# Weight halves at multiples of 512 bytes, and the first projection in another order of chunks with the compressed product's slabs between them

## The reference

```python
def hybrid_layer(h, w_in, ...):
    t = jnp.arange(S)
    hn = rms_norm(h, attn_pre_norm)
    proj = hn @ w_in                                   # 512 x 1024 @ 1024 x 2072
    (q_n, k_c, v_c, k_s, v_s, k_w, v_w, g_n, q_w, k_sw, v_sw) = jnp.split(proj, IN_SPLITS, axis=-1)
    qn = rope(kvh(q_n, NSA_HEADS), t).reshape(B, S, NSA_KV, NSA_GROUP, HEAD_DIM)
    k_c, k_s, k_w = (rope(kvh(z, NSA_KV), t) for z in (k_c, k_s, k_w))
    ckv = jax.vmap(compress)(jnp.stack([k_c, v_c]), cmp_pos, cmp_w1, cmp_w2)
    o_cmp, p_cmp = compressed_attention(qn, ckv[0], ckv[1], t)
    ...
    o_win = banded_attention(qn, k_w, v_w, NSA_WINDOW, None)
    gates = jax.nn.sigmoid(g_n)...
    qw = rope(kvh(q_w, SWA_HEADS), t)...
    kw = rope(kvh(k_sw, SWA_KV), t)
    o_swa = banded_attention(qw, kw, kvh(v_sw, SWA_KV), SWA_WINDOW, ...)
    mixed = jnp.concatenate([o_nsa, o_swa], axis=-1) @ w_out

def compress(kv, pe, w1, w2):       # overlapping blocks of 32 tokens: 31 blocks x 2 heads = 62 rows
    ...
    return jax.nn.gelu(flat @ w1) @ w2                 # flat: 62 x 2048, w1: 2048 x 256, for k and for v
```

## Time and profile before

| | |
|---|---|
| median of 3 runs | 2015.52 us (2012.99 to 2016.8) |
| the profiled execution: its time, its span | 2015.36 us, 2013.2 us |
| PE busy | 1911.2 us, 95% |
| PEld, DVE, ACT, POOL busy | 1519.0, 797.1, 470.6, 1081.5 us |
| mean granted clock of TensorE | 0.983 |
| chain that ended last | PE 86%, DVE 7%, ACT 4%, POOL 1%, DMA 1% |

### The profile page before, as it was taken

How to read it: one execution, slowest core, us unless ns; L and a number is a source line. 1 busy time by engine, 2 the same in 40 slices (tenths; PEclk the granted TensorE clock), 3 DMA queues, 4 the chain that set the end, 5 groups by cost and what they waited for, 6 DMA issues and landing times.

```text
span 2013.2 us, 28099 instructions
## 1 busy us (share of the span) xinstructions
PE 1911.2 (95%) x10416; PEld 1519.0 (75%) x10416; DVE 797.1 (40%) x1283; ACT 470.6 (23%) x1144; POOL 1081.5 (54%) x713
## 2 busy tenths in 40 slices
PE   8968899999999989988999999999998899999999
PEld 6857567888888877756888888887885688888887
DVE  5445655756662055663332232013527333222200
ACT  2115543322220043453210010011326221001000
POOL 7454125666665555252566666665534456666663
PEclk9988999999999999999999999999999999999999
DMA  4221012233232322210322332223221023332222
GB/s 160 76 88 33 2 33 84 84 95 93 94 104 84 101 72 77 62 44 22 95 92 93 93 94 94 92 79 85 84 63 34 32 84 94 94 94 94 94 94 84
DMA packets 121501, 159.50 MB, mean 79 GB/s; under 512 B 8514, under 2 KB 83778, under 8 KB 121409
## 3 DMA queue, kind: packets, MB, share of 16 engines
q1 hardware_dynamic: 121409, 158.21, 25.6%
HBM read 155.04 MB, written 2.10 MB: 78 GB/s over the span
## 4 chain that ended last, share of the span: by engine, by line
PE 86%; DVE 7%; ACT 4%; issue 1%; POOL 1%; DMA 1%; SPq 0%; DVEq 0%; POOLq 0%; ACTq 0%
PE ps L814 25%; PE ps L815 25%; PE ps L816 25%; PE ps L1187 3%; PE ps L1160 1%; PE ps L829 1%; DVE p_turn L2298 1%; DVE nmax L2264 1%; PE ps L1234 1%; ACT dump L1524 1%; ACT tok L1764 1%; PE ps L962 1%; ACT xt_hi L1543 1%; PE ps L1264 1%; PE ps L1250 1%
## 5 line engine op out<-in xcount | busy, mean ns | idle before, releaser
L457 POOL TENSOR_TENSOR w_lo<-raw,w_hi 128x1024 fp32r<-128x1024 f32 (+1 forms) x256 | 606.5, 2369 | 21.3
L455 POOL TENSOR_SCALAR w_hi<-raw 128x1024 fp32r<-128x1024 f32 (+1 forms) x256 | 267.5, 1045 | 551.1 <-PE ps L816 515.6
L814 PE MATMUL ps<-xt_hi,w_hi 128*128 128x512 f32 (+2 forms) x1096 | 427.1, 390 | 0.9 <-ACT tok L1932 0.9
L815 PE MATMUL ps<-xt_lo,w_hi 128*128 128x512 f32 (+2 forms) x1096 | 426.3, 389 | 0.0
L816 PE MATMUL ps<-xt_hi,w_lo 128*128 128x512 f32 (+2 forms) x1096 | 426.2, 389 | 0.0
L814 PE MATMUL ps<-w_hi,xt_hi 128*128 128x512 f32 (+3 forms) x672 | 263.3, 392 | 18.5 <-DVE tok L2413 12.8
L815 PE MATMUL ps<-w_lo,xt_hi 128*128 128x512 f32 (+3 forms) x672 | 258.9, 385 | 0.0
L816 PE MATMUL ps<-w_hi,xt_lo 128*128 128x512 f32 (+3 forms) x672 | 258.9, 385 | 0.0
L2103 DVE TENSOR_TENSOR ps<-ps,gains 128x512 f32<-128x512 f32 x132 | 92.1, 698 | 395.3 <-PE ps L816 395.3
L814 PEld LDWEIGHTS ps<-xt_hi,w_hi 128*128 128x128 f32 (+1 forms) x1096 | 206.0, 188 | 48.7 <-POOL w_lo L471 1.3
L815 PEld LDWEIGHTS ps<-xt_lo,w_hi 128*128 128x128 f32 (+1 forms) x1096 | 205.9, 188 | 47.5
(11 more groups left out here) (318 smaller groups left out, 2203.7 us busy)
## 6 DMA issues: line engine op xcount, KB each, us to landing
raw<-in_w_up SPq DMA_DIRECT2D x88, 256.0 KB
raw<-in_l_w_gate SPq DMA_DIRECT2D x88, 256.0 KB
raw<-in_l_w_up SPq DMA_DIRECT2D x88, 256.0 KB
raw<-in_l_w_down SPq DMA_DIRECT2D x40, 512.0 KB
raw<-in_l_w_in SPq DMA_DIRECT2D x36, 512.0 KB
raw<-in_w_down SPq DMA_DIRECT2D x20, 512.0 KB
raw<-in_l_w_o SPq DMA_DIRECT2D x16, 512.0 KB
raw<-in_w_in SPq DMA_DIRECT2D x12, 512.0 KB
```

The costliest lines, as they stand in the source:

```text
L455: e.tensor_scalar(w_hi[:, s, 0:width], r, 1.0, 0.0, ALU.mult, ALU.add).then_inc(split, 1)
L457: e.tensor_tensor(w_lo[:, s, 0:width], r, w_hi[:, s, 0:width].bitcast(F32), ALU.subtract).then_inc(split, 1)
L814: e.matmul(o, s_hi, m_hi, start=start, stop=False)
L815: e.matmul(o, s_hi, m_lo, start=False, stop=False)
```

## The change

1. Tensors. A tensor `align_h` of 384 bytes stands ahead of `h`, `rot` moves to another place, and the filler `align_x` grows. `raw` now starts at byte 33,280, `w_hi` at 41,472 and `w_lo` at 57,856, all multiples of 512; the tensors from `m_table` on, `xt` and `hid` among them, stay where they were.
2. The chunks of the first projection come in the order: compressed and second keys and values (`C_KV`, 512), sliding-window keys and values (`C_SK`, 256), queries (`C_Q`, 512), sliding-window queries (`C_SQ`, 512), window keys and values with the gates (`C_WIN`, 280). The two short key chunks are staged in `mixed` (`tok_short`) instead of `tok`.
3. The eight slabs of the compressed product stand one by one behind slab 3 of `C_Q`, the four of `C_SQ` and the first three of `C_WIN`, in the programs of SP, POOL and PE.
4. Of the eight banks, four hold the tiles, three the turns, and bank 7 the compressed product. The turns are at other places, and those of `C_WIN` (two, written to `kk[:, 2:4]`) go into rounds 4 and 6 of the attention, their copies into rounds 5 and 7 of ACT.
5. In DVE's program the rows for the compressed product stand behind the turn of `C_KV`; the gates' three operations go into round 3 of the attention. In ACT's program the GELU and its table loads stand ahead of the copies of `C_WIN`.
6. The attention's start waits for two tiles of `C_WIN` (`in1_tok` 18), its round 1 for all four.

```diff
-ALIGN = 12
+ALIGN = 44
...
+    sb("align_h", [P, 96])
     h = sb("h", [P, NT, D])
...
     sb("align_x", [P, ALIGN])
-    rot = sb("rot", [P, 4 * ROPE])
...
-    IN1 = [(0, 512), (512, 512), (1024, 280), (1304, 512), (1816, 256)]
+    IN1 = [(512, 512), (1816, 256), (0, 512), (1304, 512), (1024, 280)]
+    C_KV, C_SK, C_Q, C_SQ, C_WIN = range(5)
+    CMP_SLABS = [(kv, s) for kv in range(2) for s in range(4)]
+    ORDER1 = []
+    for c in range(5):
+        for s in range(4):
+            ORDER1.append(("in", c, s))
+            if 11 <= len([x for x in ORDER1 if x[0] == "in"]) - 1 < 19:
+                ORDER1.append(("cmp", *CMP_SLABS[len([x for x in ORDER1 if x[0] == "cmp"])]))
+    N1 = {x: n for n, x in enumerate(ORDER1)}
...
-    TOK_BANKS = {"in1": EVEN, "in2": EVEN, "in3": HIGH}
-    TURN_BANKS = {"in1": ODD, "in2": ODD, "in3": LOW}
+    TOK_BANKS = {"in1": (0, 1, 4, 5), "in2": EVEN, "in3": HIGH}
+    TURN_BANKS = {"in1": (2, 6, 3), "in2": ODD, "in3": LOW}
...
+    def pe_in1(e, plan):
...
+        turned = {(C_Q, 0): C_KV, (C_Q, 2): C_SK, (C_SQ, 2): C_Q, (C_WIN, 2): C_SQ}
+        for n, (kind, c, s) in enumerate(ORDER1):
+            e.wait_ge(split, 2 * (n + 1))
+            if kind == "cmp":
+                compressed(c, s).then_inc(slab_used, 1)
                 continue
...
             for t in range(NT):
+                if s == 0 and c:
+                    e.wait_ge(*at("in1_tok", 4 * c - 3 + t))
+                m = tile(c, s, t)
+            m.then_inc(slab_used, 1)
+            if (c, s) in turned:
+                pe_turn(e, "in1", plan, turned[c, s], [at("in1_tok", 4 * turned[c, s] + 4)])
...
+        def banks_there():
+            e.wait_ge(*at("in1_tok", 20))
+            e.wait_ge(*at("in1_copy", 12))
+            turned_layer()
...
-        hooks = {1: turned_layer, 3: second_layer, 5: lambda: scores(0), 7: lambda: scores(1), 11: lambda: turned(0),
+        hooks = {1: banks_there, 4: lambda: window_key(0), 6: lambda: window_key(1), 8: window_there, 3: second_layer, 5: lambda: scores(0), 7: lambda: scores(1), 11: lambda: turned(0),
...
+        for step in (C_KV, C_SK, (C_KV,), "high", (C_SK,), (C_Q,), (C_SQ,), "layer", C_WIN):
...
+        for step in (C_KV, C_SK, (C_KV,), "rows", (C_SK,), C_Q, (C_Q,), C_SQ, (C_SQ,), C_WIN):
+            if step == "rows":
                 block_rows()
                 block_rows_low()
...
         hooks, variance = dve_cat()
+        hooks.setdefault(3, []).append(gates)
```

More of the change, by code:

```diff
@@ L347, in n_slot, with sp_group @@
         return SLOT[0] % 2
-    def sp_group(e, grp, slabs, stride=W, first=0):
+    def sp_group(e, grp, slabs, stride=W):
         STRIDE[0] = stride
-        for s, parts in enumerate(slabs, first):
+        for s, parts in enumerate(slabs):
             SLOT[0] = s
@@ L397, in _ @@
         e.dma_start(g_pre[:, :, :], A["g_pre"]).then_inc(sem("g_full"), 16)
[L398 to L411, removed]
+        for n, (kind, c, s) in enumerate(ORDER1):
+            if kind == "in":
+                parts, STRIDE[0] = two_kt(A["w_in"][0], *IN1[c])[s], W
+            else:
+                parts, STRIDE[0] = [(0, cols(A["cmp_w1"][0, c], 0, 256, slice(4 * s, 4 * s + 4)))], 256
+            SLOT[0] = n
+            sp_slab(e, n, parts)
+            if n == 1:
+                e.dma_start(smalls[:, :], A["smalls"]).then_inc(sem("small_full"), 16)
+                e.dma_start(pos_i[:, :], A["positions"]).then_inc(sem("small_full"), 16)
+                e.dma_start(table[:, :], A["table"]).then_inc(sem("small_full"), 16)
         for c in range(2):
@@ L697, in _ @@
         ph = phases
[L698 to L701, removed]
+        for n, (kind, c, s) in enumerate(ORDER1):
+            if kind == "in":
+                split_cols(e, n // 4, n % 4, 2, IN1[c][1])
+            else:
+                split_slab(e, n // 4, n % 4, SLAB)
         pool_first(e, {3 + 4 * s: (ph["out1"].g0, s) for s in range(4)})
@@ L821, in pe_turn, with tile, compressed @@
             for s, v in tok_waits:
                 e.wait_ge(s, v)
-        for i, (cc, (off, w, _, _), _, _) in enumerate(plan):
-            if cc != c:
+        for i in units:
+            pe_turn_unit(e, name, plan, i)
+    def pe_in1(e, plan):
+        def tile(c, s, t):
+            n = N1["in", c, s]
+            for k in range(2):
+                hi, lo = x_model(2 * s + k, t)
+                cs = slice(k * W, k * W + IN1[c][1])
+                m = mm3(e, bank(TOK_BANKS["in1"][t], IN1[c][1]), hi, lo, w_hi[:, n % 4, cs], w_lo[:, n % 4, cs],
+                        s == 0 and k == 0, s == 3 and k == 1)
+            if s == 3 and t < 3:
+                m.then_inc(sem("in1_acc"), 1)
+            return m
+        def compressed(kv, s):
+            n = N1["cmp", kv, s]
+            if s == 0:
+                e.wait_ge(*at("cmp_f", kv + 1))
+            for k in range(4):
+                pp = 4 * s + k
+                cs = slice(k * 256, (k + 1) * 256)
+                m = mm3(e, bank(7, 256, 256 * kv, 62), f_hi[:, kv, pp, :], f_lo[:, kv, pp, :], w_hi[:, n % 4, cs],
+                        w_lo[:, n % 4, cs], pp == 0, pp == CMPS - 1)
+            return m
+        turned = {(C_Q, 0): C_KV, (C_Q, 2): C_SK, (C_SQ, 2): C_Q, (C_WIN, 2): C_SQ}
+        for n, (kind, c, s) in enumerate(ORDER1):
+            e.wait_ge(split, 2 * (n + 1))
+            if kind == "cmp":
+                compressed(c, s).then_inc(slab_used, 1)
@@ L2420, in _, with rotate @@
         e.wait_ge(*od.latest())
-        for c in range(5):
+        def rotate(c):
             for t in range(NT):
```

177 lines of the change are left out of this document (92 added, 85 removed).

## The result

The changed kernel takes 1958.63 us (median of 4 runs, 1958.28 to 1962.69) where the kernel before takes 2014.26 in the same comparison (4 runs). The ratio is 0.9727, 95% interval 0.971 to 0.9745. The forecast was 1996.3, range 1986 to 2004: the direction held, the time did not. The change gained 55.6 us, not 19.1.

A forecast was written before the change was run, and what follows sets the result against it. TensorE was taken as the bound, working 1911 of 2013 us. 22.6 of waits + 4.2 of clock - 3.1 + 0.9 = 24.6, less 5.5 in the attention, gives 19.1; 2015.4 - 19.1 = 1996.3 us, range 1986 to 2004.

The forecast's parts named there:

- Part 4: Moving tensors to 512-byte starts gains 0; bounds: 63 us gained at a 213 ns step, or 6.9 us lost.
- starts quicken matmuls: Rival: starts at 512 speed up matmuls, 1989 us at 1 ns each, down to 1933; chance 0.08.
- slower: Rival: weights and activations 256 bytes apart modulo 512 collide more, 2024 us at 4 ns a matmul; chance 0.04.
- The order, 19.1 us: Whole forecast gain: 24.6 us won up to the attention less 5.5 us that the attention takes over.
- Waits removed, 22.6 us: PE's waits in the first 155 us: 12.8 for VectorE's tiles, 8.0 for compressed slabs, 1.8 the view hides.
- The clock at 105 to 122 us, 4.2 us: PE's work from 112.1 to 122.2 us ran at 1.2 GHz; at 2.4 GHz it takes 4.2 us less.
- No wait; the slack is 1 to 3 us: First query chunk: rows end at 72 us, its tiles rotate until 81.2, and PE gets its banks in time.
- Chunk 0 to 1, 1.0 and 1.1; the 280-wide chunk, 1.0: New PE waits for banks: two after the key/value chunk, one before the 280-wide chunk; 3.1 us in all.
- GpSimd and loads in the last chunk, no wait: Slabs between chunks: with three slabs of lead PE never waits for GpSimd; bound 0 to 3 us.
- The start of the attention, 2.9: First exponentials come 5.0 us after PE's projections instead of 2.1, behind table loads, copies and rotations: cost 2.9 us.
- Gates, evictions, transposes, 2.7: Work moved into the attention: gates 0.9 us, two window-key evictions 0.6, eight transposes 1.2.
- The clock stays up in the attention: Rival: the clock no longer falls early in the attention, worth some 6 us, so 1990 us; chance 0.17.

The follow-up runs named there:

- starts alone: The kernel before with only the tensors' places of the changed one, order of work as before: 1980.41 us, ratio 0.9829.
- slabs at the end: The changed kernel with the eight compressed slabs behind all five chunks and the GELU behind the last chunk's copies: 1967.1 us, ratio 0.9774.
- order alone: The changed kernel with the tensors where they were before, so only the order of work differs from the kernel before: 1994.95 us, ratio 0.9888.
- rows in two: The changed kernel with the keys' rows in place and the values' rows moved behind the first query chunk's rotation: 1957.14 us, ratio 0.972.
- the worst: The changed kernel with the rows in two parts and GELU with table loads behind the last chunk's copies: 1960.7 us, ratio 0.9731; attention 127.9 us.
- 32 apart: The changed kernel with raw, w_hi and w_lo 224 past a multiple of 512, xt and hid 256 past: 1995.27 us, ratio 0.9903.
- 64 apart: The changed kernel with raw, w_hi and w_lo 192 past a multiple of 512, xt and hid 256 past: 1985.30 us, ratio 0.9856.

## Why the prediction was wrong, point by point

- **Part 4, "I take 0, by these two": wrong, and nearly all of the miss of 37.7 us.** The step was "128 and 256 past are alike". In both rows one operand lies 128 past and the other 256 past a multiple of 512: they are the same case twice, 128 apart, with the roles exchanged. Equal rows said nothing on the start, since neither had any other distance. The measured term is 6.1 ns on 6,384 matmuls, 39 us by the steps, 34.5 us by the kernel with the starts alone. The rival "starts quicken matmuls" (0.08) was what happened, with 1 ns where it is 6; "slower", which named the distance modulo 512 as the danger, had the right quantity with the wrong sign. The 16-byte lines of the Trainium skill ("SBUF — State Buffer", "Door 1: The DMA port swizzle") gave 0 as well and don't show this.
- **The order, 19.1 us: right in size, in part by luck.** It is 22.6 us by the ratio (18 to 27) and 18.0 between the profiled executions. But two misses cancel: by the first exponential 17.1 us were won (18.2 between the kernel with the starts alone and the changed one) where the sum had 21.7, and what the attention was to take over behind it, 2.7 us, didn't show (see below).
- **Waits removed, 22.6 us: right.** Both groups went; the kernel with the slabs at the end got its 8.4 us back.
- **The clock at 105 to 122 us, 4.2 us: the spell went**, but 3.4 us of low clock came at 80.6, half of them lost.
- **"No wait; the slack is 1 to 3 us" at the first query chunk: wrong.** The term of the sum was the block's length, taken as 12.5 us plus 1.3 and measured as 17.3 (59.20 to 76.5). 7.9 us of splits lay beside the rows, not 5, and VectorE lost nearly all of them, not 0.6 of each us: (14.98 - 10.22) / (7.9 - 2.7) = 0.9, with 2.7 us of splits beside them before. The 0.6 was an average over three short splits in which one operation had started first and kept its time; the pair of 1.88 us in the earlier trace rows already ended behind a split (the first of the two at 104.92, the split at 104.56). The first tile was out at 79.2 us; PE, which wanted it at 77.05, waited 2.3 us and had another 1.7 of low clock. Here the exclusive lock of the Trainium skill ("SBUF — State Buffer", "SBUF: two separate sides") was the better forecast, as the pair at 64.21 shows; it gave a wait of 1.4 us, and 17.7 for the sum.
- **Chunk 0 to 1, 1.0 and 1.1; the 280-wide chunk, 1.0: right.** Two waits of 0.87 by the view, each 0.16 longer by the start-to-start, and one of 0.60, likewise.
- **GpSimd and loads in the last chunk, no wait: right.** GpSimd waited for a load up to 2.12 us a slab, more than the 0.6 that I walked with, and PE never for GpSimd.
- **The start of the attention, 2.9: 2.2.** The first exponential came 4.3 us after PE's last projection, against 2.1. It came at 134.2 us, 19.9 earlier than before; my walk said 130, my own sum 24.6 - 2.9 = 21.7 earlier, 132.4. The walk and the sum didn't agree and I didn't notice. The sum was the better: 21.7, less 4.0 at the query chunk, plus 0.7 here, is 18.4, and the starts give 1.7 by then (the first exponential of the kernel with the starts alone): 20.1.
- **Gates, evictions, transposes, 2.7: no such cost shows.** With the order alone the attention takes 1.5 us longer than before, but with 3.4 us more of low clock, worth 1.3 at 0.37 for each; the changed kernel's is 1.5 us shorter than that of the starts alone, with 3.4 us less. Both leave about 0.2 us, one dearer and one cheaper. (The sum's own parts, 2.9, 0.9, 0.6 and 1.2, make 5.6 and not 5.5.)
- **The clock stays up in the attention (0.17):** it fell again in the changed kernel. In the trace of the kernel with the rows in two it fell for 3.4 us and later for 6.8, and its attention is 3 us shorter than this one's, 10 shorter than the worst.

## What to carry to other kernels

Before a property is taken as free because two rows agree, write out its value for both operands in each row, and look whether the rows differ in the combination that could matter. Here, for matmuls of 512 columns in this format, stationary and moving operand should start alike modulo 256 bytes, which a filler of some hundred bytes does. A VectorE operation with two SBUF inputs that would start beside a GpSimd split should be costed to the end of the split, and a block of many short ones by the time that GpSimd leaves free. And a gain of 3 us ahead of a stage in which the clock wavers isn't seen in the time; read it from the trace at the stage's start.

## What the chip showed that I had not expected

- The step of a 512-column matmul of these halves is 226.9 ns when all starts are alike and up to 233.3 otherwise; no kernel came nearer to the 213 ns of the prediction's bound. At 384 columns (176 to 174 ns from before to changed) and at 416 (190 to 188) the step fell too, but other kernels break the order: 32 apart has 174 ns at 384, and the order alone 187 at 416. At 256 and 280 columns (120 and 128 ns) the starts change a nanosecond or so, but for 114 ns at 256 columns with `w` streaming in the kernel 64 apart, and with 16 stationary columns (231.5 ns at 512) nothing.
- The out-of-step cost isn't smooth: 32 bytes apart costs 6.4 ns, 64 apart 2.0 or 6.4 by which operand is stationary, 128 apart 6, 256 nothing.
- A table load of ACT took 1.28 us in every row.
